# Down-projection weight sums: raw blocks copied inside HBM, sums stored in two parts from ScalarE's stream, up weights issued by SyncE

## What is computed

```python
D_MODEL, SEQ, D_FF = 1024, 1024, 4096          # float32 throughout

x = x + g_m * y
h = rms_norm(x, norm_mlp[i]) * (1 + sc_f) + sh_f
x = x + g_f * (jnp.square(jax.nn.relu(h @ w_mlp_in[i])) @ w_mlp_out[i])
```

## Time and profile before

| | us |
|---|---|
| median of 3 runs | 2793.88 (2791.40 to 2798.71) |
| the profiled execution, its own time | 2793.08 |
| its span in the trace | 2791.3 |
| output projection ends, up-projection begins on TensorE | 736.47 |
| down-projection's first matmul | 1209.26 |
| TensorE busy over the span | 2605.0 |
| granted TensorE clock, mean | 0.975 |

### The profile page before, as it was taken

The page is one execution under the profiler, slowest core; times in us unless marked ns, Lnnn a source line. Parts: engine busy times, 40 slices in busy tenths (PEclk is TensorE's granted clock), DMA queues, the critical chain, the costliest instruction groups (busy, mean ns, idle before and its releaser), DMA issues. The chain is left out here.

```text
span 2791.3 us, 55669 instructions
## 1 busy us (share of the span) xinstructions
PE 2605.0 (93%) x22330; PEld 1878.7 (67%) x22330; DVE 1637.7 (59%) x4094; ACT 876.9 (31%) x2171; POOL 305.9 (11%) x411
## 2 busy tenths in 40 slices
PE   6999999999989889899999989999999899999996
PEld 4888856664677767778788657777777655544443
DVE  5443267775555655645556338888888756422225
ACT  3211056651322212211101136666666500200002
POOL 0000033310000000000000001111111100543312
PEclk9999999999999999999999999999999899999998
DMA  6010044420256668687987720000000030799995
GB/s 243 32 61 31 12 157 153 133 93 31 91 213 259 241 231 293 249 324 292 360 314 292 288 83 29 5 27 29 29 3 29 18 117 31 257 397 400 400 372 203
DMA packets 138259, 476.06 MB, mean 171 GB/s; under 512 B 11152, under 2 KB 20880, under 8 KB 129056
## 3 DMA queue, kind: packets, MB, share of 16 engines
q1 hardware_dynamic: 125440, 416.54, 40.3%
q10 hardware_dynamic: 4320, 31.46, 3.0%
q0 software_dynamic: 8256, 24.65, 2.4%
HBM read 375.55 MB, written 97.06 MB: 169 GB/s over the span
## 5 line engine op out<-in xcount | busy, mean ns | idle before, releaser
L2202 PE MATMUL mixing_ps<-all_main,pre_ws 64*64 64x256 f32 x3072 | 247.7, 378 | 0.0
L3289 PE MATMUL ex_ps<-all_main,ex_xT 128*128 128x512 f32 x496 | 223.2, 593 | 3.0 <-DVE ex_xT L3447 2.1
L1340 PE MATMUL mlp_ps<-all_main,all_early 128*128 128x256 f32 x512 | 132.8, 405 | 40.1 <-DMA all_early<-in_w 37.5
L3289 PEld LDWEIGHTS ex_ps<-all_main,ex_xT 128*128 128x128 f32 x496 | 91.7, 190 | 107.5 <-issue 102.3
L1511 ACT ACTIVATE all_gates<-all_gates 128x256 f32<-128x256 f32 x128 | 52.5, 410 | 305.6 <-DVE all_gates L1566 288.2
L2202 PEld LDWEIGHTS mixing_ps<-all_main,pre_ws 64*64 64x64 f32 x3072 | 134.0, 134 | 19.6 <-issue 0.7
L1340 PEld LDWEIGHTS mlp_ps<-all_main,all_early 128*128 128x128 f32 x512 | 101.2, 201 | 61.9 <-DMA all_early<-in_w 44.2
L1340 PE MATMUL mlp_ps<-all_tail,mlp_w2s 128*128 128x256 f32 x512 | 126.5, 404 | 14.3 <-issue 14.2
L254 PE MATMUL qkv_ps<-qkv_wq,h_hT 128*128 128x256 f32 x576 | 133.0, 383 | 2.9 <-DVE h_hT L547 2.9
L1340 PEld LDWEIGHTS mlp_ps<-all_tail,mlp_w2s 128*128 128x128 f32 x512 | 105.1, 206 | 33.6 <-issue 14.7
L1382 PE MATMUL mlp_ps<-mlp_w2s 128*128 128x256 f32 x448 | 126.2, 383 | 0.0
(11 more groups left out here) (512 smaller groups left out, 5618.6 us busy)
## 6 DMA issues: line engine op xcount, KB each, us to landing
all_main<-in_w_gu SPq DMA_DIRECT2D x31, 2048.0 KB, 14.8
t_rows<-all_xres SPq DMA_DIRECT2D x16, 3136.0 KB, 11.3
mlp_w2s<-t_rows SPq DMA_DIRECT2D x56, 896.0 KB, 6.8
all_early<-in_w ACTq DMA_DIRECT2D x30, 1024.0 KB, 7.2
all_early<-t_rows SPq DMA_DIRECT2D x28, 896.0 KB, 6.2
all_tail<-t_rows SPq DMA_DIRECT2D x28, 896.0 KB, 5.5
att_wa<-in_w_ada SPq DMA_DIRECT2D x32, 512.0 KB, 3.9
all_early<-in_w_d SPq DMA_DIRECT2D x16, 1024.0 KB, 17.4
```

The costliest lines, as they stand in the source:

```text
L1340: last = nc.tensor.matmul(ps[:, bank(n, name), 0:QB], lhsT=weights(k), rhs=moving(k), start=k == 0, stop=k == HK - 1)
L2202: last = nc.tensor.matmul(ps[heads(m), banks[half], 0:UT], lhsT=ws[heads(half), n, k, heads(m)], rhs=columns(k, heads(half)), start=(k == ...
L3289: last = nc.tensor.matmul(pg[:, n % 2, :], lhsT=(xT[:, n % 2, :] if x is None else x)[:, k * P:(k + 1) * P], rhs=gu[n][:, k, :], start=(k ...
```

## The change

1. **Raw blocks.** The nine raw blocks of each step no longer pass through SBUF. Sixteen DMAs copy them from w2 to `t_rows` inside HBM, 128 x 3 rows of 384 floats (1536 bytes) each, 576 KB a DMA. SP issues them behind `pair_weights(1)` and ahead of the parking of x.
2. **Two stores.** The rest is stored in two DMAs: the three raw inner blocks of the four outer sums (4 x 384 floats a partition, 768 KB) after the outer sums, and the four inner sums of all seven outer blocks (7 x 512 floats, 1792 KB) after the inner sums. Each has a semaphore of its own (`outer_out`, `within_out`), which DVE waits for before it overwrites that part.
3. **Who issues.** Sub loads and both stores move to ACT, each behind the squared corner given by `MADE_BEFORE`. The load of the next slice waits for the sums, not for the store, and stands ahead of the second store. The up weights move to SP, which waits and issues in its own sequence.
4. **Spreading.** The four parts of `sub_sums` stand at positions 0, 3, 5, 7 of a step instead of 0, 1, 2, 3. The four weight sums of the next pair stand one each behind c22, c11, c21 and c12.
5. **Hidden rows.** They are read back behind the even ring loads 40 to 54 and the odd ring loads 49 to 63.

```diff
-        sub_steps = {made_from(s) + n: (s, n) for s in range(SUBS) for n in range(4)}
-        sub_stores = {made_from(s) + 5: s for s in range(SUBS)}
-        sub_loads = {made_from(s - 1) + 8 if s else 10: s for s in range(SUBS)}
+        STEP_AT = (0, 3, 5, 7)
+        MADE_BEFORE = {"c22": (0, 1, 2, 3), "c11": (4,), "c21": (5,), "c12": (6,)}
+        sub_steps = {made_from(s) + STEP_AT[n]: (s, n) for s in range(SUBS) for n in range(4)}
...
                 pair_weights(sp, 0)
                 pair_weights(sp, 1)
+                for k in range(SUBS):
+                    sp.dma_start(t_rows[0:3, k // 2, :, k % 2, 0:3 * P].rearrange("o p n -> p o n"),
+                                 w2[k // 2, k % 2, :, 0:3, 1:4, :].rearrange("p o i n -> p o (i n)")).then_inc(raw_out, 16)
                 sp.wait_ge(xn_done, TT)
                 for t in range(TT):
                     sp.dma_start(x_rows[t * P:(t + 1) * P, :], xres[:, t, :]).then_inc(parked, 16)
-                for n in range(2 * FPAIRS):
-                    for i in range(7):
-                        at = 7 * n + i
-                        if at in sub_stores:
-                            sub_store(sub_stores[at])
-                        if at in sub_loads:
-                            sub_load(sub_loads[at])
-                        if i == 3 and n > FPAIRS:
-                            hidden_store(n - 1)
...
+                for n in range(1, 2 * FPAIRS):
+                    if n + 1 < 2 * FPAIRS:
+                        pair_weights(sp, n + 1)
+                    if n > FPAIRS:
+                        hidden_store(n - 1)
+                    if n == 2 * FPAIRS - 2:
+                        sp.wait_ge(outer_out, 16 * SUBS)
+                        sp.wait_ge(within_out, 16 * SUBS)
+                        for t in range(TT):
+                            sp.dma_start(xres[:, t, :], x_rows[t * P:(t + 1) * P, :]).then_inc(x_back, 16)
...
-                    if 5 * QUADS + 6 <= n < 6 * QUADS + 6:
-                        hidden_load(0, n - 5 * QUADS - 6)
-                    if 6 * QUADS + 6 <= n < 7 * QUADS + 6:
-                        hidden_load(1, n - 6 * QUADS - 6)
+                    if 5 * QUADS <= n < 7 * QUADS and n % 2 == 0:
+                        hidden_load(0, (n - 5 * QUADS) // 2)
+                    if 6 * QUADS <= n < 8 * QUADS and n % 2 == 1:
+                        hidden_load(1, (n - 6 * QUADS) // 2)
...
+                def sub_load(s):
+                    if s:
+                        act.wait_ge(sub_made, 8 * s)
+                    else:
+                        act.wait_ge(parked, 16 * TT)
+                    act.dma_start(sub_all[:, 0:3, 0:4, :], w2[s // 2, s % 2, :, 0:3]).then_inc(sub_in, 16)
+                    act.dma_start(sub_12, w2[s // 2, s % 2, :, 3]).then_inc(sub_in, 16)
+
+                def sub_transfers(s, n):
+                    if n == 1:
+                        act.wait_ge(sub_made, 8 * s + 4)
+                        act.dma_start(t_rows[3:7, s // 2, :, s % 2, 0:3 * P].rearrange("o p n -> p o n"),
+                                      sub_all[:, 3:7, 1:4, :].rearrange("p o i n -> p o (i n)")).then_inc(outer_out, 16)
+                    if n == 3:
+                        if s + 1 < SUBS:
+                            sub_load(s + 1)
+                        act.wait_ge(sub_made, 8 * s + 8)
+                        act.dma_start(t_rows[:, s // 2, :, s % 2, 3 * P:7 * P].rearrange("o p n -> p o n"),
+                                      sub_all[:, :, 4:8, :].rearrange("p o i n -> p o (i n)")).then_inc(within_out, 16)
...
                         n = half * FPAIRS + j
-                        if 1 <= n < 2 * FPAIRS - 1:
-                            pair_weights(act, n + 1)
                         act.wait_ge(up, up_at(n, "m1"))
...
                             nc.scalar.activation(out, corner[name], ACT.Square).then_inc(squared, 1)
+                            if n == 1 and name == "c22":
+                                sub_load(0)
+                            for i in MADE_BEFORE[name]:
+                                if 7 * n + i in sub_steps:
+                                    sub_transfers(*sub_steps[7 * n + i])
...
                     add(n, "c22", corner["c22"], "m5", u3)
-                    if n + 1 < 2 * FPAIRS:
-                        every(sums_of(n + 1))
+                    next(next_sums, None)
                     between(4)
                     corner_free("c11")
                     add(n, "c11", corner["c11"], "m2", first_copy)
+                    next(next_sums, None)
...
                     add(n, "c21", corner["c21"], "m4", u3)
+                    next(next_sums, None)
...
                     add(n, "c12", corner["c12"], "m3", u4)
+                    next(next_sums, None)
```

More of the change, by code:

```diff
@@ L1099, in stage_out_mlp @@
         summed, tokens, whole, copied, ended = (s.sem(n) for n in "summed tokens whole copied ended".split())
-        clamped, parked, sub_in, sub_made, sub_out = (s.sem(n) for n in "clamped parked sub_in sub_made sub_out".split())
+        clamped, parked, sub_in, sub_made = (s.sem(n) for n in "clamped parked sub_in sub_made".split())
+        raw_out, outer_out, within_out = (s.sem(n) for n in "raw_out outer_out within_out".split())
         hid_out, hid_in, x_back = [s.sem("hid_out0"), s.sem("hid_out1")], [s.sem("hid_in0"), s.sem("hid_in1")], s.sem("x_back")
@@ L1202, in _ @@
             def _(sp):
-                def sub_load(s):
-                    if s:
-                        sp.wait_ge(sub_out, 16 * s)
-                    else:
-                        sp.wait_ge(parked, 16 * TT)
-                    sp.dma_start(sub_all[:, 0:3, 0:4, :], w2[s // 2, s % 2, :, 0:3]).then_inc(sub_in, 16)
-                    sp.dma_start(sub_12, w2[s // 2, s % 2, :, 3]).then_inc(sub_in, 16)
-                def sub_store(s):
-                    sp.wait_ge(sub_made, 8 * s + 8)
-                    sp.dma_start(t_rows[:, s // 2, :, s % 2, :].rearrange("o p n -> p o n"),
-                                 sub_all[:, :, 1:8, :].rearrange("p o i n -> p o (i n)")).then_inc(sub_out, 16)
                 def hidden_store(n):
@@ L1558, in tokens_of @@
                     yield nc.vector.tensor_tensor(T4, B21, T2, ALU.subtract).then_inc(tokens, 1)
-                def every(steps):
-                    for _ in steps:
-                        pass
                 def add(n, name, out, product, other):
@@ L1602, in corner_free @@
                             dve.wait_ge(squared, square_at(n - 1, name))
+                    next_sums = sums_of(n + 1) if n + 1 < 2 * FPAIRS else iter(())
                     between(0)
```

10 lines of the change are left out of this document (4 added, 6 removed).

## The result

The changed kernel takes 2748.69 us in the median of 4 runs (2746.9 to 2758.72), the kernel before 2796.3 beside it (2791.4 to 2804.06). The ratio is 0.9835 with a 95% interval of 0.9801 to 0.9868: 1.65% faster, some 48 us. The profiled execution of the changed kernel is its slowest of the four, 2758.72 with a span of 2757.0; a second profiled execution (first experiment) took 2750.32. One of the five executions of the kernel in "Loads that don't wait, alone" took 5321.61 us, for no reason that the record shows, and is left out of its ratio.

What follows compares the result with a forecast made beforehand. Bound: the up-projection loses 82.4 us to late slices, late up weights and clock. Loss left 56.1 (copies 48.1, late phase 4, entry 4), read-backs gain 4: gain 30.3, from 2793.88 to 2764 us; range 2740 to 2796.

Steps and rivals of the forecast that it cites:

- the rival with fast copies: HBM copies ahead of pair 2 take 30 us, as piece prices say; gain 47.3, kernel 2747 us; chance 0.20.
- the late phase: Up-projection, s = 3, 7, 11, 15: late slice loads make weights late at four places, 2.4 to 11 us, taken as 4.
- the entry: Start of the down-projection: waits of 1.47 and 1.41 us, untouched, and a bit of clock; 4 us of loss stay.
- The raw copies: Sixteen HBM copies in SP's queue ahead of x and pair 2's weights: delay 45.8 plus slow start 2.3, 48.1 us.
- T: Time of the 9.44 MB of HBM copies, taken as 47 us; pair 2 starts late by T - 1.2.
- The chain of waits: Up-projection: a slice load waiting for a store delays DVE, then sums, corners and ACT's weight issue; one late slice costs twice.
- Up weights on SP: Up-projection: SP issues about 1.4 us into the next pair, landing at 8.6, at worst 10.8, both before 12.09.
- Spread sums: DVE in the up-projection: same instructions, corners no longer behind four weight sums; nothing added to the gain.
- four DMAs on ACT: ACT issues four DMAs a step, some 1.7 us in 21; costs nothing unless it blocks.
- Read-backs: Down-projection: hidden rows spread over 24 ring loads instead of 16; gain 4 us, between 0 and 6.
- Stalls stay: Rival: late weights come from sharing DMA engines; half the up-projection waits stay, gain 5, 2789 us; chance 0.16.
- Slow copies: Rival: HBM copy rows bound by round trip; no gain at T = 77, 2817 us at 100; chance 0.14.

Runs made afterwards that it cites:

- first experiment: The changed kernel measured once more, nothing altered: 2749.50 us, ratio 0.9835 to the kernel before.
- Loads that don't wait, alone: Against the kernel before: slice loads by SP wait for sums only, hidden HBM copies, two stores a step, up weights still on ACT: 2779.92 us, ratio 0.9939.
- the last run: Against the changed kernel: copies first, pair 2's weights ahead of parking x, x read back behind eight down-projection ring loads: 2719.48 us, ratio 0.9738.
- sums together: Against the changed kernel: step parts back at positions 0, 1, 2, 3 and the four weight sums together behind c22: 2747.48 us, ratio 0.9839.

## Why the prediction held, point by point

The forecast was 2764, the time 2748.69, inside the range and in the direction that had 0.70. It is nearly the number of the rival with fast copies, 2747, and that rival's mechanism is the one that happened; but the sum meets the time by errors that partly cancel: the copies are put 20 us too dear, the late phase and the entry 9 too cheap.

*The raw copies: the term that was mis-sized.* The choice of T = 47 rested on "A copy touches it twice, 18.9 MB, 47 us at 400". The copies took 30 us, T = 30 as the piece prices said, with 76.5 ns a piece in the mean against their 77. The delay with the slow start is 27.6 against 48.1: 20.5 too much, of which 17 are T; the rest is that the copies began 1.4 us earlier than put down and that 12.8 us lay behind them instead of 15.4, less 0.5 for a slower start. A ceiling seen in rows with one side in SBUF was carried to a case that none of them shows. The piece price was the better row, and it was met partly by luck: the 40 ns were read as the price of 512 bytes but are a mean over two sizes. The kernel before from 522.0 to 523.4, when the pieces are of 2048 bytes, and from 523.5 to 525, when nearly all are of 512 (pieces, MB, share of 16 engines):

```profile
q1 hardware_dynamic: 176, 0.36, 77.0%
```

```profile
q1 hardware_dynamic: 914, 0.49, 107.1%
```

That is 98 and 28 ns, and a line between those gives 75 for 1536 bytes. The Trainium skill's 214 GB/s a direction ("DMA: Bandwidth & Descriptors", section "Latency and other measured facts"), cited there, was measured on rows of 16 KiB in another layout; these copies ran at 340.

The measured 27.6 are not all the copies' either. 20.4 went when they were moved; 4.4 of gap and about 3 of slow start are there without them, as x now stands ahead of pair 2's weights in SP's queue. The sum has no term for that: with T = 0 it would have pair 2 start on time.

*The chain of waits: right in a part, not the whole root.* "So one late slice costs twice" made the slice the root. The three worst pairs of the kernel before bear it out: pairs 12, 19 and 26, each with a wait of DVE for its slice in it or just ahead of it, have ACT's three latest issues (11.8, 16.1 and 13.7 us in) and 33.9 of the 82.4 us. No run takes away DVE's late steps and leaves the rest, since the run meant for it moved them to a wait for stores. But they are not needed for late weights: with issues 4.7 and 5.1 us into the pair in the median, and DVE's waits for slices down to 31.3 and 29.6 us, TensorE still stood for weights in eleven places and in ten. And they don't suffice: DVE's wait for slices, foretold to fall to about 20, rose to 54.1, and with the sums spread and the weights on SP it cost little. In the kernel before the issue came 6.3 us in, in the median, plus 7.2 to land: more than the 12.09 of a pair. ACT issued behind the corners, and what made the corners late made the weights late. The prediction took 3.4 from pair 1, which has no step of slices yet, and thought ACT late only where DVE was. How the 82.4 us divide between the two stays open.

*Up weights on SP: the decisive part, and better than foretold.* 0.2 us into the pair, not 1.4. The prediction, and "The kernel before" with it, has `pair_weights(n + 1)` wait for the sums of pair n; the code waits for those of pair n - 1, which read the buffer that is overwritten, and they were made a pair earlier. Landing 6.4 later the weights are there 5.5 ahead of need, and the slowest (10.2) still 1.7 ahead. This is also why late slices do little harm now. But it works only in a queue without slices and stores: alone it is worth nothing (1.0009), without it the rest is worth nothing (1.0021).

*The late phase, 4 us.* No weight comes late there. What stays outside the gap and the entry is 10.9, in 7.1 of short issue waits and in clock: 7 more than the term.

*Entry of the down-projection, 4.* 6.1 in the stage and 0.9 behind its first product. It goes when x's loads go elsewhere (the last run), and also when they go out some 8 us earlier against the pairs (sums together), so "untouched" was wrong: the spread last step moved them.

*Spread sums, four DMAs on ACT: nothing.* Right in total. For the sums it is 6 us gained within the pairs and 6 lost at the entry; alone, in the kernel before, they cost 14. ACT's DMAs have no run of their own.

*Read-backs, 4.* Right, by the mean of thirteen traces, though the trace after shows only 0.6.

Summed again with what was measured, the loss left is 27.6 + 10.9 + 6.1 = 44.6, the gain 82.4 - 44.6 + 4 = 41.8, which from 2793.88 gives 2752; the median is 2749.

*The rivals.* Stalls stay: refuted, the weights' only wait is the gap, although the traffic in the second half is nearly as high as it foresaw (289 GB/s and 0.80 of the engines' time from 961.95 to 1153, against its 303). Slow copies: refuted, the gap is 24.8 and not over 76.

## What to carry to other kernels

For a load that a bottleneck engine needs, work out two numbers from the trace before anything else: how far into its period it is issued, and how long it takes to land; if they add up to more than the period, move the issue to a stream that has nothing to wait for and a queue that holds nothing large. A wait on another engine, however large its total, is not the root until a run without it says so. And a large transfer that nobody needs soon costs by what stands behind it in its queue: the same 9.4 MB cost 20.4 us or nothing, by their place in the order. Last, when a run takes one wait away, look what its engine waits for at the same place now: a wait can come back under another name.

## What the runs showed of the hardware

A copy from HBM to HBM in rows of 1536 bytes ran at 340 GB/s, read and written at once, at 75 to 77 ns a row on each of 16 engines. That is what loads of 512- and 2048-byte pieces give on a line between them, 75: the second side in HBM cost nothing visible. Like steps with like traffic differ by the queue: from issue to landing a 1024 KB load took 11.5 us in the mean of twelve behind a large store in its own queue, and 8.3 when that was in the other one. And a pair that began behind an idle TensorE lost 2.8 us after 24.8 idle and 3.0 after 4.4; in the first 5 us the granted clock was 0.50 both times.
